# Hybrid decoder step on one core: who copies the second own strides, where head 2's rotation and head 3's sums stand, and the order of the first softmax work

## The chip, the cores and the metric

The kernel runs on one core of a Trainium2 chip. The metric is the device time of one execution in microseconds. Before the change three executions took 855.06, 856.63 and 857.32 us, median 856.63 us.

## What is computed

One layer of a decoder trunk for 512 prompt tokens and 64 sample tokens (8 sequences of 8, each with 1024 cached rows): a root-mean-square norm, one input projection, a convolution branch and a sparse attention branch, their gated sum, then a mixture of 32 experts. What the change touches lies in the attention branch: the rotation of the queries, and the compression of raw keys and values.

```python
def rope(x, pos):
    ...
    return jnp.concatenate([x1 * cos - x2 * sin, x2 * cos + x1 * sin], axis=-1).astype(x.dtype)

def compress(k_raw, w1, b1, w2):
    ...
    pre = jnp.einsum('bnlgd,lde->bnge', s[:, 0:nb], w1r[0]) + b1
    for r in range(1, CMP_RATIO):
        pre = pre + jnp.einsum('bnlgd,lde->bnge', s[:, r:r + nb], w1r[r])
    return jnp.einsum('bnge,ef->bngf', jax.nn.silu(pre), w2)
```

Compression runs twice, first for keys and then for values. Each time 16-row strides are multiplied by two matrices (w1), neighbouring strides are added, a silu follows, and a second small matrix (w2). The attention then takes compressed scores (31 per query in the prompt), selected blocks and a window. Each of the eight query heads is rotated for the last two.

## The kernel before, in words

Every engine has its own program, written by hand. What passes from TensorE through PSUM to VectorE or ScalarE is a job in one list, ORDER (lines 66 to 75). There are four PSUM slots of 1024 columns, and a job's place in the list modulo four is its slot. claim (a wait of TensorE) lets a job start when the job four places earlier has been emptied, take waits for it to be filled, and result_of waits for it to be emptied. So the order of the list, and each engine's own order, set who waits for whom.

The jobs around the change are these:

- raw (n, u), with n = 0 for keys and 1 for values: TensorE turns half a block of 128 cached strides (raw_turned, L1964). Four copies of 64x512 put the result into XT (spread, L819). For n = 1 VectorE copies u = 4 and u = 6, and ScalarE the other six.
- own (n): the prompt's own 32 strides are turned (own_turned, L1973) and copied in four pieces of 64x256 (spread_own, L827). ScalarE copies them for n = 0 and VectorE for n = 1.
- w1 and w1own (n): compress_first multiplies the cached strides (32 matmul instructions at L1983, 512 columns each) and the own ones (32 at L1989, 32 columns each). It waits until raw 4 to 7 and own are copied. ScalarE copies the upper half out (upper_halves, L1069 and L1072), VectorE adds (compress_pre, L1417 and L1424), ScalarE applies silu (compress_silu, L1076). w2 is the second product (L2040 and L2041 for keys, L2058 for values; w2own is at L2063).
- q (c): queries projects a pair of heads, c from 0 to 3 (L1886); ScalarE copies it out (L1081, L1082). "Head c" below is this pair.
- rope (c): TensorE permutes the queries (rotated, L2001). VectorE makes two products (L1431, L1433, the second empties the slot) and two sums: L1435 writes the prompt's rotated queries qrot, L1436 the samples' qs. All rotations share the scratch tile qtmp.

The convolution is VectorE's: conv (L1376) for the prompt, conv_sample (L1402, L1404) in eight steps of one multiplication and one reduction for the samples, and its bias (L1408). SyncE and GpSimd wait for the end of the convolution (conv_done) before they start loads for the stage after the attention (GpSimd's first is L943).

The prompt's attention starts when the last four jobs before it are empty. TensorE computes the compressed scores (cmp_scores, L2128 and L2130) and the scores of units 0 and 1 (L2094, L2097); there are 24 units, six to a head. VectorE takes the compressed maxima (cmp_maxima, L1523, L1524), the units' maxima (maxima, L1498) and the compressed sums and weights (cmp_normalize, L1528 to L1532), and weights the units' probabilities (normalize, L1503 to L1508). ScalarE takes exponentials (L1136 and L1131). cmp_turns (L2136) needs cmp_normalize; behind it TensorE computes unit 2's scores and then turns unit 0's probabilities (L2107). A unit's scores need qrot of its head only, and head 3 comes with unit 18. qs is read by GpSimd after the whole attention.

Of the kernel before, what the change touches and what calls it, by code (L numbers as in the profile page):

```python
# [20 lines left out]
SEQ, DB, DS = 512, 8, 8  # L21
# [41 lines left out]
def mg_jobs(n0, n1):  # L63
# [4 lines left out]
ORDER += [("gs", 0), ("ga", 0), ("raw", 0, 0), ("kt", 0), ("gs", 1), ("raw", 0, 1), ("ga", 1), ("raw", 0, 2), ("kt", 1),  # L68
          ("gs", 2), ("raw", 0, 3), ("ga", 2), ("raw", 0, 4), ("gs", 3), ("raw", 0, 5), ("ga", 3), ("raw", 0, 6), ("raw", 0, 7), "cso"]
ORDER += [("own", 0), ("q", 0), ("w1", 0), ("w1own", 0), ("raw", 1, 0), ("raw", 1, 1), ("q", 1), ("w2", 0), ("rope", 0),  # L70
          ("raw", 1, 2), ("raw", 1, 3), ("q", 2), ("raw", 1, 4), ("raw", 1, 5), ("rope", 1), ("raw", 1, 6), ("raw", 1, 7), ("own", 1), ("rope", 2),
          ("w1", 1), ("w1own", 1), ("q", 3), ("w2", 1), "w2own", ("rope", 3)]
J_ATT = len(ORDER)
ORDER += [("keys", 0, 0), ("keys", 0, 1)] + mg_jobs(0, 4) + ["mean"] + mg_jobs(4, 8) + [("keys", 0, 2)] + mg_jobs(8, 10) + ["var"] + mg_jobs(10, 22)
ORDER += [("small", 0), ("mg", 22), ("mg", 23), ("pcn", 0), ("mg", 24), ("imp", 0), ("mg", 25), ("head", 0), ("mg", 26)]
# [12 lines left out]
JOB = {name: n for n, name in enumerate(ORDER)}  # L88
# [37 lines left out]
def build(nc, a):  # L126
    o = a["outs"]
    with ExitStack() as ctx:
# [36 lines left out]
        def take(eng, *jobs, it=None, per=0):  # L165

            highest(eng, filled, [want(j, it, per, 1) for j in jobs])

        def result_of(eng, *jobs, it=None, per=0):

            highest(eng, emptied, [want(j, it, per, 1) for j in jobs])
# [4 lines left out]
        def give(ins, j):  # L176
            ins.then_inc(emptied[home_of(j)[0]], 1)
# [644 lines left out]
        def spread_own(copy, how, j):  # L822

            for q in range(2):
                for g in range(NKV):
                    v = slot(j)[g * HD:(g + 1) * HD, 0:512].rearrange("p (k q s) -> p k q s", q=2, s=STR_P)[:, :, q, :]
                    last = copy(XT[q * HD:(q + 1) * HD, g, :, STR_S:STR], v, *how)  # L827
            return last
# [199 lines left out]
        def _(act):  # L1028
# [26 lines left out]
            def spread_raw(n, *us):  # L1055
                for u in us:
                    j = JOB["raw", n, u]
                    take(act, j)
                    give(spread(nc.scalar.activation, (ACT.Copy,), j, u), j)
# [6 lines left out]
            def upper_halves(n):  # L1066
                j = JOB["w1", n]
                take(act, j)
                nc.scalar.activation(upper[:, :, 0:STR_S], slot(j)[HD:P, :].rearrange("p (g n) -> p g n", g=NKV), ACT.Copy).then_inc(s_upper, 1)  # L1069
                j = JOB["w1own", n]  # L1070
                take(act, j)
                nc.scalar.activation(upper[:, :, STR_S:STR], slot(j)[HD:P, 0:2 * STR_P].rearrange("p (g n) -> p g n", g=NKV), ACT.Copy).then_inc(s_upper, 1)  # L1072
# [19 lines left out]
            j = JOB["cso"]  # L1092
# [9 lines left out]
            spread_raw(1, 2, 3)  # L1102
            queries(2)
            spread_raw(1, 5, 7)
            upper_halves(1)
            compress_silu(1)
            queries(3)
# [203 lines left out]
        def _(dve):  # L1311
# [75 lines left out]
            def spread_raw(n, u):  # L1387
                j = JOB["raw", n, u]
                take(dve, j)
                give(spread(V.tensor_copy, (), j, u), j)  # L1390

            def conv_sample(t0, t1):

                if t0 == 0:
                    dve.wait_ge(s_anew, CC)
                    result_of(dve, JOB["ga", CC - 2], JOB["ga", CC - 1])
                weights = wdw[:, :, :].unsqueeze(2).to_broadcast([P, CC, DB, TAPS])
                new = cv[:, :, SEQ:T].rearrange("p c (b t) -> p c b t", t=DS)
                for t in range(t0, t1):
                    if t:  # L1400
                        dve.wait_ge(s_prod, 2 * t)
                    V.tensor_tensor(cprod, aS[:, :, :, t:t + TAPS], weights, ALU.mult).then_inc(s_prod, 1)  # L1402
                    dve.wait_ge(s_prod, 2 * t + 1)
                    V.tensor_reduce(new[:, :, :, t], cprod, AX.X, ALU.add).then_inc(s_prod, 1)  # L1404
                if t1 == DS:
                    dve.wait_ge(s_prod, 2 * DS)
                    for c in range(CC):
                        V.tensor_scalar(cv[:, c, SEQ:T], cv[:, c, SEQ:T], bdw[:, c:c + 1], None, ALU.add).then_inc(s_conv, 1)  # L1408

            def compress_pre(n):  # L1410
                j = JOB["w1", n]
                dve.wait_ge(s_pads, 3)
                take(dve, j)
                dve.wait_ge(s_upper, 2 * n + 1)
                for g in range(NKV):
                    lo = slot(j)[0:HD, g * 512:(g + 1) * 512].rearrange("p (b n) -> p b n", b=DB)
                    last = V.scalar_tensor_tensor(pre[:, g, 0:STR_S].rearrange("p (b n) -> p b n", b=DB)[:, :, 0:NCS], lo[:, :, 0:NCS], b1[:, n:n + 1],  # L1417
                                                  upper[:, g, 0:STR_S].rearrange("p (b n) -> p b n", b=DB)[:, :, 1:NCS + 1], ALU.add, ALU.add)
                give(last, j)
                j = JOB["w1own", n]  # L1420
                take(dve, j)
                dve.wait_ge(s_upper, 2 * n + 2)
                for g in range(NKV):
                    last = V.scalar_tensor_tensor(pre[:, g, STR_S:STR_S + NCP], slot(j)[0:HD, g * STR_P:g * STR_P + NCP], b1[:, n:n + 1],  # L1424
                                                  upper[:, g, STR_S + 1:STR_S + 1 + NCP], ALU.add, ALU.add)
                give(last, j)

            def rotated(c):
                j = JOB["rope", c]
                result_of(dve, JOB["q", c])  # L1430
                st.do(V.tensor_tensor(qtmp[:, 1, :], qT[:, c, :], cosT[:, :], ALU.mult))  # L1431
                take(dve, j)
                give(V.tensor_tensor(halves(qtmp[:, 0, :]), tokens(j), halves(sinT[:, :]), ALU.mult), j)  # L1433
                result_of(dve, j)
                V.tensor_tensor(qrot[:, c, :], qtmp[:, 0, 0:SEQ], qtmp[:, 1, 0:SEQ], ALU.add).then_inc(s_qrot, 1)  # L1435
                st.do(V.tensor_tensor(qs[:, 1, c, :], qtmp[:, 0, SEQ:T], qtmp[:, 1, SEQ:T], ALU.add))  # L1436

            j = JOB["cst"]
            take(dve, j)
# [35 lines left out]
            rotated(0)  # L1475
            conv(3, 22, TAPS)
            spread_raw(1, 4)
            rotated(1)
            spread_raw(1, 6)
            j = JOB["own", 1]  # L1480
            take(dve, j)
            give(spread_own(V.tensor_copy, (), j), j)
            rotated(2)
            conv_sample(0, 5)
            compress_pre(1)
            conv_sample(5, DS)
            j = JOB["w2own"]
            take(dve, j)
            for g in range(NKV):
                r = slice(g * STR_P, (g + 1) * STR_P)  # L1490
                last = V.tensor_copy(vcB[r, g * HD:(g + 1) * HD], slot(j)[r, g * HD:(g + 1) * HD])
            give(last, j)
            rotated(3)

            def maxima(u):
                x = unit[u]
                dve.wait_ge(s_score, u + 1)
                V.tensor_reduce(x.stat(0), x.by_branch(x.scores), AX.X, ALU.max, negate=True).then_inc(s_max, 1)  # L1498
# [27 lines left out]
            def cmp_normalize(c):  # L1526
                dve.wait_ge(s_cexp, c + 1)
                st.do(V.tensor_reduce(cstat[c][:, 1, :], Pc[c % 2], AX.X, ALU.add))  # L1528
                st.do(V.reciprocal(cstat[c][:, 1, :], cstat[c][:, 1, :]))
                g = gates[:, 0:QT, :].rearrange("p q (g c r) -> p q g c r", g=NKV, c=HPG)[:, :, :, c, 0]  # L1530
                st.do(V.tensor_tensor(cstat[c][:, 2, :].rearrange("p (q g) -> p q g", g=NKV), cstat[c][:, 1, :].rearrange("p (q g) -> p q g", g=NKV), g, ALU.mult))
                V.tensor_tensor(Pc[c % 2], Pc[c % 2], wide_c(cstat[c][:, 2, :]), ALU.mult).then_inc(s_cnorm, 1)  # L1532

            cmp_maxima(0)
            maxima(0)
            maxima(1)
            cmp_normalize(0)
            normalize(0)
            for u in range(NU):
                if u + 2 < NU:  # L1540
                    maxima(u + 2)
                if u + 1 < NU:
                    normalize(u + 1)
                if u % PER_C == 2 and u // PER_C + 1 < HPG:
                    cmp_maxima(u // PER_C + 1)
                probs_turned(u)
                if u % PER_C == 4 and u // PER_C + 1 < HPG:
                    cmp_normalize(u // PER_C + 1)
# [328 lines left out]
        def _(pe):  # L1877
# [89 lines left out]
            def own_turned(n):  # L1967
                j = JOB["own", n]
                src = (raw[0], raw_own)[n]
                pe.wait_ge(*((s_raw[0], 48) if n == 0 else (s_own, 16)))  # L1970
                claim(pe, j)
                for k in range(16):
                    last = tr(slot(j)[:, k * STR_P:(k + 1) * STR_P], src[0:STR_P, k, :], ident[0:STR_P, 0:STR_P])  # L1973
                fill(last, j)
# [72 lines left out]
            rotated(1)  # L2047
            raw_turned(1, 6, 7)
            own_turned(1)
            rotated(2)  # L2050
            compress_first(1)
            queries(3)
            j = JOB["w2", 1]
            pe.wait_ge(s_silu, 2)
# [457 lines left out]
```

## Time and profile before

| | before |
|---|---|
| median of 3 executions | 856.63 us |
| the profiled execution | 858.87 us |
| its span, first to last instruction | 857.0 us |
| mean granted TensorE clock | 0.951 |
| TensorE busy | 754.0 us (88%) |
| VectorE busy | 380.0 us (44%) |
| ScalarE busy | 220.8 us (26%) |
| GpSimd busy | 167.0 us (19%) |

Times in the trace are microseconds from the first instruction. In the rows PE is TensorE's matrix products, PEld its weight loads, DVE VectorE, ACT ScalarE, POOL GpSimd and SP SyncE. "x16" is a count of instructions merged into a row, and a bracket at its end tells how long the engine was idle before it and what ended that. The granted clock is a share of full speed, so 0.50 is the lower of TensorE's two levels. The stage that the change touches lies between 185 and 250 us.

### The profile page before, as it was taken

How to read it: one execution, taken by the hardware profiler on the slowest of the kernel's cores; microseconds unless marked ns; L12 is line 12 of the kernel's file. 1: busy time of each engine (PE TensorE's matmuls, PEld its weight loads, DVE VectorE, ACT ScalarE, POOL GpSimd, SP SyncE). 2: the span in 40 equal slices, each digit the busy share in tenths (PEclk: the TensorE clock that was granted, in tenths of full speed). 3: DMA queues.
4: the chain of work that ended last, by engine and by line, in shares of the span. 5: the costliest groups of instructions: out<-in, count | busy, mean ns of one | idle time of the engine just before them, and what ended most of it. 6: DMA issues, size and time to landing. Idle time of an engine off the chain costs nothing.

```text
span 857.0 us, 11122 instructions
## 1 busy us (share of the span) xinstructions
PE 754.0 (88%) x4270; PEld 518.1 (60%) x4270; DVE 380.0 (44%) x799; ACT 220.8 (26%) x480; POOL 167.0 (19%) x270
## 2 busy tenths in 40 slices
PE   5999999998899989999999979999996499987730
PEld 3557787774666667777777657774454365554410
DVE  2213999898778861030045532222137432221118
ACT  3001233350356651251244420000010122212113
POOL 2449265000200014000024210001000223221100
PEclk9999999999999999999999999999997699999975
DMA  9766354220540005432234279104007699999836
GB/s 315 152 32 198 101 122 146 63 73 1 168 166 2 1 26 174 132 102 61 74 98 150 79 208 396 43 0 136 24 26 306 239 370 412 406 400 395 313 127 250
DMA packets 87567, 138.95 MB, mean 162 GB/s; under 512 B 25493, under 2 KB 60465, under 8 KB 86351
## 3 DMA queue, kind: packets, MB, share of 16 engines
q1 hardware_dynamic: 71503, 101.41, 34.5%
q0 software_dynamic: 11392, 32.71, 12.9%
q10 hardware_dynamic: 4616, 4.08, 1.5%
q8 instruction: 36, 0.59, 0.3%
q14 instruction: 20, 0.16, 0.1%
HBM read 132.00 MB, written 21.14 MB: 179 GB/s over the span
## 4 chain that ended last, share of the span: by engine, by line
PE 76%; DMA 10%; DVE 7%; issue 4%; SPq 2%; ACT 2%; another core or an unknown queue 0%; POOL 0%; DVEq 0%; POOLq 0%; ACTq 0%
PE ps L1886 18%; PE ps L2076 14%; PE ps L2322 6%; PE ps L2393 5%; PE ps L1910 5%; DMA keep<-w_up 4%; PE ps L1983 3%; PE ps L2409 2%; DMA arena<-w_up 2%; PE ps L2119 2%; PE ps L2107 2%; PE ps L2094 2%; PE ps L1964 2%; PE ps L2383 1%; PE ps L2174 1%
## 5 line engine op out<-in xcount | busy, mean ns | idle before, releaser
L2076 PE MATMUL ps<-xT,keep 128*128 128x288 f32 x512 | 126.9, 407 | 0.9 <-ACT h L1190 0.5
L2076 PEld LDWEIGHTS ps<-xT,keep 128*128 128x128 f32 x512 | 96.5, 190 | 27.6 <-ACT h L1190 0.9
L1886 PE MATMUL ps<-xT,arena 128*128 128x288 f32 x384 | 95.4, 407 | 0.0
L1376 DVE SCALAR_TENSOR_TENSOR cv<-keep,cv 128x512 f32<-128x512 f32 x120 | 83.6, 747 | 1.4
L1886 PEld LDWEIGHTS ps<-xT,arena 128*128 128x128 f32 x384 | 72.1, 190 | 19.2
L2322 PE MATMUL ps<-arena,xT 128*128 128x512 f32 x128 | 55.5, 593 | 1.8 <-issue 1.8
L2393 PE MATMUL ps<-keep,mgT 128*64 128x256 f32 x288 | 44.1, 406 | 9.2 <-DMA keep<-w_up 6.3
L2393 PE MATMUL ps<-arena,mgT 128*64 128x256 f32 x256 | 39.9, 397 | 4.4 <-DMA xT<-w_up 3.0
L1910 PE MATMUL ps<-mgT,xT 128*128 128x512 f32 (+1 forms) x128 | 43.2, 497 | 0.0
L2322 PEld LDWEIGHTS ps<-arena,xT 128*128 128x128 f32 x128 | 24.1, 190 | 31.4 <-issue 31.4
L1260 ACT ACTIVATE keep<-h 128x1024 f32<-128x1024 f32 (+1 forms) x5 | 5.3, 1058 | 140.3 <-DVE h L1687 131.7
L819 ACT ACTIVATE mgT<-ps 64x512 f32<-64x512 f32 x56 | 33.1, 591 | 32.0 <-PE ps L1964 31.4
L1007 POOL DMA_INDIRECT yscratch<-cv,slots_of x19 | 19.0, 999 | 109.2 <-PE ps L2383 76.7
L2393 PEld LDWEIGHTS ps<-keep,mgT 128*64 128x64 f32 x288 | 27.5, 146 | 19.7 <-issue 11.7
L1886 PE MATMUL ps<-cv,keep 128*128 128x288 f32 x128 | 34.6, 426 | 5.3 <-DMA arena<-w_nsa_out 5.3
L1837 DVE TENSOR_TENSOR arena<-ps,cv 128x128 f32<-128x128 f32 x19 | 5.5, 292 | 73.1 <-ACT cv L1275 73.1
L962 POOL TENSOR_SCALAR keep<-keep,pmod 128x64 f32<-128x64 f32 x16 | 6.8, 443 | 157.0 <-PE ps L2119 85.2
L1910 PEld LDWEIGHTS ps<-mgT,xT 128*128 128x128 f32 x128 | 24.1, 190 | 18.1 <-issue 14.8
L1114 ACT ACTIVATE mgT<-ps 128x288 f32<-128x288 f32 x32 | 13.1, 410 | 79.6 <-PE ps L2076 76.1
L1886 PEld LDWEIGHTS ps<-cv,keep 128*128 128x128 f32 x128 | 25.6, 201 | 12.9 <-issue 5.4
L1131 ACT ACTIVATE arena<-ps,arena 128x128 f32<-128x128 f32 (+3 forms) x64 | 32.9, 528 | 1.7 <-DVE arena L1498 0.9
L1275 ACT ACTIVATE cv<-ps 128x128 f32<-128x128 f32 x19 | 5.3, 277 | 108.1 <-PE ps L2393 108.1
(387 smaller groups left out, 1275.0 us busy)
## 6 DMA issues: line engine op xcount, KB each, us to landing
arena<-w_down SPq DMA_DIRECT2D x21, 512.0 KB
keep<-w_gate SPq DMA_DIRECT2D x18, 512.0 KB
keep<-w_up SPq DMA_DIRECT2D x18, 512.0 KB
keep<-w_in SPq DMA_DIRECT2D x16, 512.0 KB, 3.9
arena<-w_gate SPq DMA_DIRECT2D x14, 512.0 KB
arena<-w_up SPq DMA_DIRECT2D x14, 512.0 KB
h<-x_prompt SPq DMA_DIRECT2D x8, 512.0 KB, 7.6
arena<-w_in SPq DMA_DIRECT2D x8, 512.0 KB, 8.0
```

Source lines behind the costliest of these rows:

```text
L819: last = copy(XT[q * HD:(q + 1) * HD, g, k0:k0 + KD // 2, (u // 2) * P:(u // 2 + 1) * P], v, *how)
L1007: pool.indirect_dma_start(a["yscratch"][0:2 * T, :], bass.IndirectOffsetOnAxis(ap=slots_of[:, 1, blocks_of(p):blocks_of(p) + 1], axis=0), ...
L1131: nc.scalar.activation(x.prob[:, g, k], x.scores[:, g, k], ACT.Exp, bias=x.stat(0)[:, g, b:b + 1], accum_out=x.stat(1)[:, g, b:b + 1]).the ...
L1376: V.scalar_tensor_tensor(cv[:, c, 0:SEQ], aP[:, c, k:k + SEQ], wdw[:, c, k:k + 1], cv[:, c, 0:SEQ], ALU.mult, ALU.add).then_inc(s_tap[c], 1)
L1886: last = mm(tokens(j)[:, b, :], weights(k), halves(x[:, k, :])[:, b, :], start=k == 0, stop=k == n_k - 1)
L1910: last = mm(slot(j)[:, lo:hi], xT[:, k, i * P:(i + 1) * P], wkv[:, k, lo:hi], start=k == 0, stop=k == KD - 1)
L1964: last = tr(slot(j)[:, k * P:(k + 1) * P], raw[r % 2][:, (u % 2) * KD + k, :], ident[:, :])
L1983: last = mm(slot(j)[:, g * 512:(g + 1) * 512], w1[:, k, :], XT[:, g, k, 0:STR_S], start=k == 0, stop=k == KD - 1)
L2076: last = mm(out[:, 0:half], wmg[n // 2 % 3][:, k, :], xT[:, k, (n % 2) * half:(n % 2 + 1) * half], start=k == 0, stop=k == KD - 1, skip_gr ...
L2094: mm(x.scores[:, g, b * x.nk:(b + 1) * x.nk], qrot[hd, x.c, qc], kT[hd, br, 0:x.nk], start=b == 0, stop=False, skip_group_check=True)
L2322: last = mm(slot(j)[:, lo:lo + 512], xT[:, k, i * P:(i + 1) * P], wo[:, k, lo:lo + 512], start=k == 0, stop=k == KD - 1)
L2393: last = mm(slot(j + 1)[u * BR:(u + 1) * BR, 0:2 * F], xeT[p % 2][:, k, u * BR:(u + 1) * BR], wgu[(2 * p + u) % HOMES_W][:, :, k, :], star ...
```

## The change

- The own value strides (own 1) are copied by ScalarE, behind its raw (1, 7); VectorE's copies go.
- VectorE copies raw (1, 6) before head 1's rotation, not behind it. It runs six steps of the sample convolution, not five, before compress_pre(1), and only then head 2's rotation.
- TensorE permutes head 2 behind compress_first(1), in the job list too.
- Head 3's rotation is split: its two products stay, its two sums move to the attention, behind normalize(0).
- At the entry of the attention cmp_normalize(0) stands before maxima(1), not behind it.

```diff
--- before.py
+++ after.py
@@ -68,8 +68,8 @@
 ORDER += [("gs", 0), ("ga", 0), ("raw", 0, 0), ("kt", 0), ("gs", 1), ("raw", 0, 1), ("ga", 1), ("raw", 0, 2), ("kt", 1),
           ("gs", 2), ("raw", 0, 3), ("ga", 2), ("raw", 0, 4), ("gs", 3), ("raw", 0, 5), ("ga", 3), ("raw", 0, 6), ("raw", 0, 7), "cso"]
 ORDER += [("own", 0), ("q", 0), ("w1", 0), ("w1own", 0), ("raw", 1, 0), ("raw", 1, 1), ("q", 1), ("w2", 0), ("rope", 0),
-          ("raw", 1, 2), ("raw", 1, 3), ("q", 2), ("raw", 1, 4), ("raw", 1, 5), ("rope", 1), ("raw", 1, 6), ("raw", 1, 7), ("own", 1), ("rope", 2),
-          ("w1", 1), ("w1own", 1), ("q", 3), ("w2", 1), "w2own", ("rope", 3)]
+          ("raw", 1, 2), ("raw", 1, 3), ("q", 2), ("raw", 1, 4), ("raw", 1, 5), ("rope", 1), ("raw", 1, 6), ("raw", 1, 7), ("own", 1),
+          ("w1", 1), ("w1own", 1), ("rope", 2), ("q", 3), ("w2", 1), "w2own", ("rope", 3)]
 J_ATT = len(ORDER)
 ORDER += [("keys", 0, 0), ("keys", 0, 1)] + mg_jobs(0, 4) + ["mean"] + mg_jobs(4, 8) + [("keys", 0, 2)] + mg_jobs(8, 10) + ["var"] + mg_jobs(10, 22)
 ORDER += [("small", 0), ("mg", 22), ("mg", 23), ("pcn", 0), ("mg", 24), ("imp", 0), ("mg", 25), ("head", 0), ("mg", 26)]
@@ -1102,6 +1102,7 @@
             spread_raw(1, 2, 3)
             queries(2)
             spread_raw(1, 5, 7)
+            spread_raw_own(1)
             upper_halves(1)
             compress_silu(1)
             queries(3)
@@ -1425,15 +1426,21 @@
                                                   upper[:, g, STR_S + 1:STR_S + 1 + NCP], ALU.add, ALU.add)
                 give(last, j)
 
-            def rotated(c):
+            def rotated_parts(c):
                 j = JOB["rope", c]
                 result_of(dve, JOB["q", c])
                 st.do(V.tensor_tensor(qtmp[:, 1, :], qT[:, c, :], cosT[:, :], ALU.mult))
                 take(dve, j)
                 give(V.tensor_tensor(halves(qtmp[:, 0, :]), tokens(j), halves(sinT[:, :]), ALU.mult), j)
-                result_of(dve, j)
+
+            def rotated_sum(c):
+                result_of(dve, JOB["rope", c])
                 V.tensor_tensor(qrot[:, c, :], qtmp[:, 0, 0:SEQ], qtmp[:, 1, 0:SEQ], ALU.add).then_inc(s_qrot, 1)
                 st.do(V.tensor_tensor(qs[:, 1, c, :], qtmp[:, 0, SEQ:T], qtmp[:, 1, SEQ:T], ALU.add))
+
+            def rotated(c):
+                rotated_parts(c)
+                rotated_sum(c)
 
             j = JOB["cst"]
             take(dve, j)
@@ -1475,22 +1482,19 @@
             rotated(0)
             conv(3, 22, TAPS)
             spread_raw(1, 4)
+            spread_raw(1, 6)
             rotated(1)
-            spread_raw(1, 6)
-            j = JOB["own", 1]
-            take(dve, j)
-            give(spread_own(V.tensor_copy, (), j), j)
+            conv_sample(0, 6)
+            compress_pre(1)
             rotated(2)
-            conv_sample(0, 5)
-            compress_pre(1)
-            conv_sample(5, DS)
+            conv_sample(6, DS)
             j = JOB["w2own"]
             take(dve, j)
             for g in range(NKV):
                 r = slice(g * STR_P, (g + 1) * STR_P)
                 last = V.tensor_copy(vcB[r, g * HD:(g + 1) * HD], slot(j)[r, g * HD:(g + 1) * HD])
             give(last, j)
-            rotated(3)
+            rotated_parts(3)
 
             def maxima(u):
                 x = unit[u]
@@ -1533,9 +1537,10 @@
 
             cmp_maxima(0)
             maxima(0)
+            cmp_normalize(0)
             maxima(1)
-            cmp_normalize(0)
             normalize(0)
+            rotated_sum(3)
             for u in range(NU):
                 if u + 2 < NU:
                     maxima(u + 2)
@@ -2047,8 +2052,8 @@
             rotated(1)
             raw_turned(1, 6, 7)
             own_turned(1)
+            compress_first(1)
             rotated(2)
-            compress_first(1)
             queries(3)
             j = JOB["w2", 1]
             pe.wait_ge(s_silu, 2)
```

## Rows read from the trace of the kernel before

**Rows 1.** The page, part 4: shares of the chain that ended last.

```profile
PE 76%; DMA 10%; DVE 7%; issue 4%; SPq 2%; ACT 2%; another core or an unknown queue 0%; POOL 0%; DVEq 0%; POOLq 0%; ACTq 0%
```

**Rows 2.** The same chain in order of time, 140 to 260 us: start, duration, what.

```profile
145.57 13.73 PE ps L1983 x32
...
162.96 3.27 PE ps L1964 x16
...
176.26 1.75 PE ps L1964 x16
...
196.72 15.61 PE ps L1983 x32
212.33 3.49 PE ps L1989 x32
...
234.46 1.06 PE ps L2136 x4
235.52 1.58 PE ps L2094 x4
...
255.72 0.44 PE ps L2136 x4
...
257.18 0.84 PE ps L2094 x4
```

**Rows 3.** Waits, 140 to 260 us: waiting instruction, releaser, total, times, longest.

```profile
POOL arena L943 <- DVE cv L1408: 46.1, 1, 46.1
...
PE ps L1983 <- DVE mgT L827: 3.8, 1, 3.8
...
PE ps L2136 <- DVE arena L1532: 2.6, 1, 2.6
```

**Rows 4.** Timeline of VectorE, 190 to 248 us.

```profile
189.51 0.76 DVE L1431 TENSOR_TENSOR arena<-h,keep 128x576 f32<-128x576 f32 x1
...
191.95 2.79 DVE L819 COPY mgT<-ps 64x512 f32<-64x512 f32 x4
194.78 1.73 DVE L827 COPY mgT<-ps 64x256 f32<-64x256 f32 x4
...
198.99 1.19 DVE L1402 TENSOR_TENSOR arena<-keep 128x992 f32<-128x992 f32 x1
...
225.95 0.44 DVE L1491 COPY keep<-ps 32x64 f32<-32x64 f32 x2 [1.38 <-PE ps L2063]
```

**Rows 5.** Timeline of ScalarE, 140 to 245 us.

```profile
190.66 2.40 ACT L819 ACTIVATE mgT<-ps 64x512 f32<-64x512 f32 x4 [0.71 <-PE ps L1964]
```

**Rows 6.** The copies at L827 over the whole run: duration min/median/max.

```profile
L827 ACT ACTIVATE mgT<-ps x4: 361/376/380, 140.6 to 141.8; 64x256 f32<-64x256 f32 x4
```

**Rows 7.** Timeline of TensorE's products, 140 to 250 us.

```profile
190.56 1.18 PE L1973 MATMUL ps<-ident,arena 32*128 32x32 f32 x16
191.66 1.24 PE L2001 MATMUL ps<-h,keep 128*128 128x288 f32 x4
```

**Rows 8.** Stretches: length, busy PE, PEld, DVE, ACT, POOL, granted clock, DMA share, GB/s.

```profile
196.72:200.10 3.38, 3.38 (x4) 1.48 (x5) 3.28 (x5) 0.00 (x0) 0.00 (x0) 0.51 0.02 5
...
234.20:237.60 3.40, 3.14 (x12) 1.61 (x13) 1.46 (x8) 1.79 (x7) 0.00 (x0) 0.50 1.13 430
```

**Rows 9.** Timeline of all engines, 227.5 to 238 us.

```profile
228.00 0.69 DVE L1435 TENSOR_TENSOR h<-arena 128x512 f32<-128x512 f32 x1
...
231.35 1.82 DVE L1498 TENSOR_REDUCE arena<-ps 128x4 f32<-128x512 f32 x2 [0.59 <-PE ps L2097]
...
233.97 0.43 DVE L1532 TENSOR_TENSOR arena<-arena 128x256 f32<-128x256 f32 x1
...
234.72 0.87 DVE L1508 TENSOR_SCALAR arena<-arena 128x128 f32<-128x128 f32 x4
234.80 0.51 ACT L1131 ACTIVATE arena<-ps,arena 128x256 f32<-128x256 f32 x1
...
237.46 0.96 DVE L1498 TENSOR_REDUCE arena<-ps 128x2 f32<-128x768 f32 x1 [1.87 <-PE ps L2097]
```

## The prediction

> **What bounds the kernel now.** I read the chain that ended last first, for the engine that must get faster: TensorE holds 76% of it, VectorE 7% [rows 1]. Then the chain in order of time, to see where it leaves TensorE near the change. In the stage from 185 to 250 us the second compress product starts at 196.72 and takes 15.61 us, the own strides' part 3.49 [rows 2]. The waits say why it did not start sooner: 3.8 us on VectorE's last copy of own strides, the longest wait of TensorE here [rows 3]. The second place is the attention's entry: cmp_turns waits 2.6 us on cmp_normalize [rows 3], and later VectorE waits 1.87 us for unit 2's scores [rows 9]. The granted clock comes last, because it changes what an idle gap costs. It was 0.51 in the first 3.38 us of the product and 0.50 from 234.2 to 237.6, both times behind a stretch with no matrix product [rows 8]. The same 32 instructions took 13.73 us for keys [rows 2], so that fall cost 15.61 - 13.73 = 1.88 us. The one at the entry slowed the compressed turns and unit 2's scores to 1.06 + 1.58 = 2.64 us, where the same four turns and four 384-column score products took 0.44 + 0.84 = 1.28 for later units at full clock [rows 2]. That fall cost about 1.36.
>
> **The own copies and the product's start.** VectorE now does head 1's rotation (189.51 to 191.95, 2.44 us), raw (1, 6) (2.79) and the own copies (1.73), and is done at 196.5 [rows 4]. After the change it does raw (1, 6) from 189.51, which TensorE has turned by then (its next job on the same engine, own, starts at 190.56 [rows 7]), to 192.34, and the rotation to 192.34 + 2.44 = 194.78. ScalarE finishes raw (1, 7) at 190.66 + 2.40 = 193.06 [rows 5]. The own strides are turned at 190.56 + 1.18 = 191.74 [rows 7], so its four copies follow at once, and take 4 x 0.376 = 1.5 us, the time of the key strides' copies on ScalarE [rows 6], where VectorE's took 1.73 [rows 4]: done by 194.6. ScalarE has nothing queued behind them before the upper half of this same product, so nobody pays for its 1.5 us. The list moves too: w1 (1) now takes the slot of rope (1), which head 1's rotation empties with its second instruction, before 194.78. The product can start at about 194.85. **Term one: 194.85 - 196.72 = -1.9 us.**
>
> **Head 2's permutation.** It lies in the idle gap today, 191.66 to 192.9 [rows 7], and costs nothing. Behind the product TensorE is never idle, so its four matrix instructions come onto the path. **Term two: +1.2 us** (1.24 by its row). VectorE's side stays covered. Six sample steps are twelve instructions of 1.2 us [rows 4], so they are done near 194.8 + 14.6 = 209.4. The product ends at 194.85 + 15.6 = 210.5 or, at full clock, 194.85 + 13.7 = 208.6, and ScalarE's copy of its upper half comes between it and compress_pre. VectorE is thus late by under 0.8 us at worst, and it waits 1.38 us before w2own's copy today [rows 4]. That slack also hides head 2's rotation behind the product, which takes 2.44 us while one sample step (2.4 us) has moved ahead. If the cover went, w2own's copy, head 3's two products and the attention's start would be late one for one. In the list rope (2) takes raw (1, 7)'s slot, long empty, and q (3) keeps own's; no new slot wait falls on TensorE.
>
> **Queues.** No DMA moves in program order. GpSimd's gathers and SyncE's loads wait for the end of the convolution (GpSimd 46.1 us [rows 3]), which comes some 1 to 2 us earlier, and are used only after the attention. Price zero. Their traffic then lies against the attention's entry a little differently; TensorE reads nothing of it there.
>
> **The attention's entry.** maxima(0) and (1) fill 231.35 to 233.17, cmp_normalize ends at 234.40, normalize(0) at 235.59 [rows 9]. Unit 1's maximum reads twice the columns of unit 0's, some 1.1 of the 1.82 us. With cmp_normalize ahead of it, cmp_turns starts at about 233.35 rather than 234.46: -1.1 us for TensorE. VectorE's sum of work to the end of normalize(0) is the same, 235.59. Now the two sums of head 3 come, about 0.85 us from start to start (L1435 begins at 228.00 and took 0.69 [rows 9]; L1436 is the 64-column one, which I put at 0.2). So maxima(2) can start at 236.45. At the low clock it started at 237.46, held by TensorE [rows 9]; TensorE now has the scores at about 236.4, so both are ready together. The gain here is 237.46 - 236.45 = 1.0 us. Where the sums stood before, VectorE had to wait for TensorE anyway, so taking them away there gives nothing, and ScalarE's exponentials of unit 1, which ended at 234.80 + 0.51 = 235.3 [rows 9], end about 1 us later, still before maxima(2) is through and unit 1 is normalized. At the full clock the old order would have started maxima(2) at 237.46 - 1.36 = 236.1, and the new one still at 236.45, because VectorE now sets it: +0.35. **Term three: between -1.0 (low clock, as profiled) and +0.35 (full clock).** Which holds in a typical execution the trace cannot say; I take -0.3, half way.
>
> **The sum.** Against the profiled execution: -1.9 + 1.2 - 1.0 = -1.7, so 858.87 - 1.7 = 857.2 us with the clock's falls kept, and 855.3 if the product no longer starts slow. That execution stands 2.24 us above the median of 856.63, about what one or two such falls cost, so the typical execution probably has fewer. Against the median: -1.9 + 1.2 - 0.3 = -1.0, and the idle gap before the product shrinks from 3.8 us to 194.85 - 191.74 = 3.1. A gap of 2.6 us was enough for a fall at the entry [rows 3, 8], so 3.1 is not safe. I give the shorter gap a quarter of 1.88, some -0.4. That makes 856.63 - 1.4 = **855.2 us**. What follows the attention is tied to TensorE's progress (weights are requested when it frees their place), so the shift should arrive at the end.
>
> **A rule of the skill.** The low clock stands behind gaps of 3.8 and 2.6 us [rows 3, 8]. The Trainium skill (TensorE: Matmul & The Clock Gate, The HAM clock gate) says that "the default state is throttled, and activity releases the throttle". By that rule alone a change which shortens both gaps should keep the clock up more often; the trace agrees that falls follow gaps, and has no gap of the new lengths.
>
> **Rivals.**
>
> *Both falls vanish.* The typical execution had the fall before the product and the new one has not: -1.9 + 1.2 - 1.88, and the entry anywhere in its term, gives -2.6 - 0.3 = -2.9, so 853.7. For it: the gap shrinks by a fifth, the entry's by 1.1 of 2.6. Against it: 855.06 was the fastest of three executions, and if falls were absent there, there is nothing to gain. Chance 0.20.
>
> *The copies were not the last wait.* Something else holds the product, such as the slot that rope (1) has to leave, or ScalarE behind raw (1, 7). If VectorE's rotation starts late by 1 us, the start is 195.8, and terms one and two cancel. With the entry at +0.35 it comes out at 856.6 to 857. For it: three events (194.6, the slot, the turned strides) now meet within 1 us. Against it: each is shorter than 1.9 us late. Chance 0.15.
>
> *Slower: the clock falls in another place.* The clock fell once behind the narrow 32-column products of the keys: the next turns took 3.27 us, against 1.75 for the same 16 later, 1.5 us lost [rows 2]. In the values' run the same kind of products (3.49 us [rows 2]) were followed by full speed. Started 2 us earlier they may be the place of a fall, with head 2's permutation and head 3's query product behind them at the low level: half of a stretch like the 3.4 us of [rows 8], +1.7. With the entry at full clock that is -0.7 + 1.7 + 0.35 = +1.35 us, 858.0. It makes the change a loss as soon as more than 0.7 us is lost there, and a measurable one only where the low level lasts two such stretches: -0.7 + 3.4 + 0.35 = +3.05, 859.7. Chance 0.08, and 0.04 for the second form.
>
> **How the numbers follow.** The forecast has 0.57, the rivals 0.20, 0.15 and 0.08. A measurement of this kernel can tell about 0.3%, or 2.6 us, from no change. The forecast's bounds are -0.7 - 1.0 - 0.9 = -2.6 and -0.7 + 0.35 = -0.35, that is 854.0 to 856.3; the three executions before differ by 2.3 us among themselves. To hold 8 in 10 the range takes in most of the first two rivals: 853.3 to 857.1, with the last of its width for the scatter of a median. Faster by over 0.3% is the first rival, 0.20. Slower by over 0.3% is the third in its second form, 0.04. Within 0.3% is the rest, 0.76.
>
> **What would show it.** Right: L827 runs on ScalarE at about 193.1 to 194.6; L1983 waits about 3.0 us, on ScalarE, and starts near 194.9; L2001 stands behind L1989 and takes 1.2 us; w2own's copy starts 0.7 us earlier or, with the product at full clock, 2.6; the gap before L2136 is near 1.6 us; L1435 of head 3 stands behind the first L1508 and directly before the third L1498, with little wait between. Wrong: the product's wait ends on VectorE, at L1433; L1402 reaches past the product's end; VectorE is late at w2own; or the granted clock is down in a stretch where it was up.

## The result, and the profile after

The changed kernel takes 861.26 us, the median of 20 executions; the kernel before takes 858.23 us, also over 20. The ratio is 1.0031, with a 95% interval of 1.0018 to 1.0045: slower by about 0.3%, 2.6 us. The forecast was 855.2 us, its range 853.3 to 857.1. The value lies above the range, and the direction is wrong. (The 856.63 us that the forecast started from was the median of three executions, 1.6 us below that of 20.)

First, the changed kernel's page: the span, busy time, and the granted clock in 40 slices. TensorE's busy time grew from 754.0 to 758.5 us for the same 4270 products, and slices 10, 12 and 24 (193 to 214, 236 to 257 and 493 to 514 us) are no longer at 9, as all of the first 30 were before. The first two lie in the stage of the change.

```profile
span 857.5 us, 11122 instructions
...
PE 758.5 (88%) x4270; PEld 519.9 (61%) x4270; DVE 378.2 (44%) x795; ACT 222.2 (26%) x484; POOL 167.9 (20%) x270
...
PEclk9999999998979999999999989999997599999875
```

**What came as forecast.** Two waits of the changed kernel (columns as in [rows 3]; the first is forecast, the second, before unit 1's turns, is not and comes up below), and the timelines of ScalarE and VectorE ahead of the product. They answer to [rows 3], [rows 4] and [rows 5].

```profile
PE ps L1988 <- ACT mgT L827: 3.1, 1, 3.1
...
PE ps L2112 <- DVE arena L1519: 2.2, 2, 1.6
```

```profile
190.20 2.40 ACT L819 ACTIVATE mgT<-ps 64x512 f32<-64x512 f32 x4 [0.90 <-PE ps L1969]
192.62 1.54 ACT L827 ACTIVATE mgT<-ps 64x256 f32<-64x256 f32 x4
```

```profile
186.23 5.61 DVE L819 COPY mgT<-ps 64x512 f32<-64x512 f32 x8
191.87 0.76 DVE L1432 TENSOR_TENSOR arena<-h,keep 128x576 f32<-128x576 f32 x1
```

ScalarE copies the own strides in 1.54 us, right behind raw (1, 7), and they end TensorE's wait, which is 3.1 us now. Now the chain in order of time, which answers to [rows 2]:

```profile
194.38 16.22 PE ps L1988 x32
210.60 3.49 PE ps L1994 x32
214.09 1.05 PE ps L2006 x4
215.14 7.76 PE ps L1891 x32
```

The product starts 2.3 us earlier, but takes 16.22 us rather than 15.61, and head 2's permutation stands in the chain behind it. At 215.14 head 3's query product starts, 0.7 us earlier than the 215.82 of before. This profiled execution was 0.45 us ahead already where VectorE began raw (1, 4) (186.23 here, 186.68 before), so little of the first two terms is left.

**Where the time went.** VectorE at the attention's entry, which answers to [rows 9]:

```profile
229.74 0.69 DVE L1502 TENSOR_REDUCE arena<-ps 128x4 f32<-128x512 f32 x1
230.34 0.41 DVE L1532 TENSOR_REDUCE arena<-arena 128x8 f32<-128x256 f32 x1
...
234.61 0.69 DVE L1438 TENSOR_TENSOR h<-arena 128x512 f32<-128x512 f32 x1
235.22 0.22 DVE L1439 TENSOR_TENSOR keep<-arena 128x64 f32<-128x64 f32 x1
235.47 0.96 DVE L1502 TENSOR_REDUCE arena<-ps 128x2 f32<-128x768 f32 x1
```

cmp_normalize (L1532) follows unit 0's maximum, and the two sums (L1438, L1439) stand right in front of unit 2's maximum, with no wait between. That is the forecast's order. TensorE in the same stretch, after and then before (the bracket is the idle time ahead of a group):

```profile
227.36 0.41 PE L2133 MATMUL ps<-keep,h 128*128 128x64 f32 x2 [1.05 <-DVE arena L1434]
...
229.63 2.08 PE L2099 MATMUL ps<-keep,h 64*128 64x256 f32 x8
...
235.62 0.92 PE L2099 MATMUL ps<-keep,h 64*128 64x384 f32 x4 [0.42 <-ACT arena L1132]
...
238.36 1.06 PE L2112 MATMUL ps<-ident,arena 128*128 128x128 f32 x8 [1.61 <-DVE arena L1519]
...
241.93 2.08 PE L2099 MATMUL ps<-keep,h 64*128 64x512 f32 x4
```

```profile
228.12 0.41 PE L2128 MATMUL ps<-keep,h 128*128 128x64 f32 x2 [1.05 <-DVE arena L1433]
...
230.38 1.14 PE L2094 MATMUL ps<-keep,h 64*128 64x256 f32 x8
...
237.93 0.92 PE L2094 MATMUL ps<-keep,h 64*128 64x384 f32 x4
...
240.35 1.07 PE L2107 MATMUL ps<-ident,arena 128*128 128x128 f32 x8 [1.30 <-DVE arena L1515]
...
242.99 1.13 PE L2094 MATMUL ps<-keep,h 64*128 64x512 f32 x4
```

The wait that matters is the one before unit 1's turns (L2112 after, L2107 before): 1.61 us for 1.30. It ends on L1519, VectorE's copy of unit 0's turned probabilities, which in VectorE's order stands behind the two sums, unit 2's maximum and the weighting of unit 1. The turns still start 2.0 us earlier than before. But unit 4's scores, four matrix instructions of 512 columns, then take 2.08 us where they took 1.13. The stretches by the clock, before and after (columns as in [rows 8]):

```profile
180.00:200.00 20.00, 16.01 (x84) 11.69 (x83) 18.34 (x29) 7.45 (x14) 0.00 (x0) 0.92 0.17 53
...
240.00:250.00 10.00, 9.65 (x88) 6.39 (x88) 7.50 (x18) 4.53 (x13) 0.00 (x0) 1.00 0.40 147
```

```profile
180.00:200.00 20.00, 16.53 (x82) 11.48 (x81) 19.33 (x26) 8.33 (x17) 0.00 (x0) 0.83 0.11 46
...
240.00:250.00 10.00, 10.00 (x56) 6.63 (x56) 4.16 (x10) 3.29 (x11) 0.00 (x0) 0.50 0.37 141
```

From 240 to 250 us the clock is at its lower level throughout, where the kernel before had full speed, and in ten microseconds TensorE gets through 56 instructions rather than 88. This profile also has an earlier fall, from about 229.8 to 233.2 us, ahead of the waits discussed here: unit 1's scores (the eight instructions of 256 columns above) took 2.08 us for 1.14. The end of the attention, as the start of the merge gates in the chain (before, then after):

```profile
320.30 15.52 PE ps L2076 x64
```

```profile
323.01 15.52 PE ps L2081 x64
```

From the first compressed scores to this point: 320.30 - 228.12 = 92.18 us before, 323.01 - 227.36 = 95.65 after. The changed kernel entered the attention 0.8 us earlier and left it 2.7 us later. Its span ends only 0.5 us behind, because the profiled execution of before lost 2.9 us in the sample pairs (445 to 494 us), partly to a wait on a queue that the trace does not name; the profiles of the changed kernel and of every experiment take 46.7 us for the same stretch, that one 49.6. Why is open. One pair of profiles is therefore not enough, and the experiments go by 12 executions each and by the mean granted clock that every execution reports.

### The profile page after: what moved, and what is told of

It is laid out like the page before. It is cut to its first block, busy times and chain, and to the rows that moved or that the text cites. A ratio compares the mean times of both kernels' runs of the same rounds, so it can differ in the third digit from the quotient of the medians.

```text
span 857.5 us, 11122 instructions
## 1 busy us (share of the span) xinstructions
PE 758.5 (88%) x4270; PEld 519.9 (61%) x4270; DVE 378.2 (44%) x795; ACT 222.2 (26%) x484; POOL 167.9 (20%) x270
## 4 chain that ended last, share of the span: by engine, by line
PE 79%; DMA 8%; DVE 6%; issue 3%; SPq 2%; ACT 1%; ACTq 0%; DVEq 0%; POOLq 0%
PE ps L1891 18%; PE ps L2081 15%; PE ps L2398 6%; PE ps L2327 6%; PE ps L1915 5%; PE ps L1988 3%; PE ps L2414 3%; PE ps L2124 2%; DMA arena<-w_up 2%; PE ps L2099 2%; PE ps L2112 2%; DMA keep<-w_up 2%; PE ps L2388 2%; PE ps L2179 1%; PE ps L1969 1%
## 6 DMA issues: line engine op xcount, KB each, us to landing
arena<-w_down SPq DMA_DIRECT2D x21, 512.0 KB, 16.8
```

## The experiments

Each kernel ran 12 times, in three sets on three chips, with 35 executions of the kernel before in each set (medians 859.64, 858.60 and 858.34 us). "Mean" and "clock" are averages over a kernel's executions of the time and of the granted clock. The kernel before has a clock of 0.9462, 0.9465 and 0.9466 in the three sets and means of 859.45, 858.78 and 858.75 us. The standard error of a mean is 0.4 to 0.8 us.

| kernel | median us | ratio to before (95%) | mean minus before's | clock |
|---|---|---|---|---|
| changed, first measurement | 861.26 | 1.0031 (1.0018 to 1.0045) | +2.6 | 0.9427 |
| e1: entry order alone | 856.55 | 0.9969 (0.9951 to 0.9988) | -3.2 | 0.9492 |
| e2: deferred sums alone | 858.95 | 1.0006 (0.9983 to 1.0029) | +0.3 | 0.9453 |
| e3: the product's part alone | 858.78 | 0.9993 (0.9971 to 1.0015) | -0.3 | 0.9444 |
| e4: both entry edits | 861.21 | 1.0030 (1.0007 to 1.0052) | +1.9 | 0.9437 |
| e5: changed, sums put back | 857.24 | 0.9980 (0.9960 to 1.0001) | -1.6 | 0.9461 |
| e6: changed, sums later | 856.13 | 0.9972 (0.9954 to 0.9991) | -2.6 | 0.9477 |
| e7: changed, gap filled | 856.37 | 0.9974 (0.9954 to 0.9995) | -2.3 | 0.9492 |
| e8: e5, product's gap filled | 855.99 | 0.9963 (0.9942 to 0.9983) | -3.0 | 0.9497 |
| e9: own copies and entry order | 855.65 | 0.9961 (0.9943 to 0.9978) | -3.0 | 0.9479 |
| e10: e9, product's gap filled | 855.42 | 0.9965 (0.9949 to 0.9980) | -3.5 | 0.9487 |
| e11: e10, entry gap filled too | 855.14 | 0.9958 (0.9940 to 0.9977) | -4.0 | 0.9497 |
| e12: changed, again | 861.30 | 1.0036 (1.0015 to 1.0056) | +2.8 | 0.9417 |

(One execution of e6, at 1344.45 us, is left out of its mean and its clock. Its median has it.)

**First set: the parts alone.** Theory A was that the new order of the entry lets the clock fall, B that the sums do, C that the product's part does.

e1, only the order of the entry:

```diff
             maxima(0)
+            cmp_normalize(0)
             maxima(1)
-            cmp_normalize(0)
             normalize(0)
```

> Alone: cmp_normalize(0) ahead of maxima(1). Theory A (the new order of the entry leaves TensorE idle before unit 1's turns, and the granted clock falls there and stays down for some 10 us): slower than before by 2 to 5 us, mean granted clock over the runs lower by about 0.006, and the profile shows a low stretch between 235 and 260 us. Theory B (the head 3 sums on VectorE do it): within 1 us of before. Theory C (the product's part does it): within 1 us of before.

Theory A as stated is refuted: this edit alone makes the kernel faster by 3.2 us, and the mean clock is higher, 0.9492 for 0.9462. TensorE's timeline:

```profile
228.44 0.41 PE L2128 MATMUL ps<-keep,h 128*128 128x64 f32 x2 [1.05 <-DVE arena L1433]
...
237.89 1.06 PE L2107 MATMUL ps<-ident,arena 128*128 128x128 f32 x8 [0.78 <-DVE arena L1515]
```

Unit 1's turns start 9.45 us behind the first compressed scores, for 12.23 before, and the wait ahead of them is 0.78 us. cmp_turns starts 4.34 us behind them (232.78), for 6.34 before: 2.0 us earlier, where the forecast had 1.1. Part of that is a wait which [rows 9] does not show, because both maxima are merged in one row. In e3, which keeps the old order, VectorE waits 0.70 us between unit 0's maximum and unit 1's, for unit 1's scores:

```profile
232.39 1.23 DVE L1496 TENSOR_REDUCE arena<-ps 128x4 f32<-128x1024 f32 x1 [0.70 <-PE ps L2095]
```

The new order puts cmp_normalize(0) into that wait.

e2, only the deferral (rotated(3) split, and the sums behind normalize(0)):

```diff
-            rotated(3)
+            rotated_parts(3)
...
             normalize(0)
+            rotated_sum(3)
```

> Alone: head 3's two sums behind normalize(0). Theory A: within 1 us of before. Theory B: slower than before by 2 to 5 us with a lower mean clock, because maxima(2) and all of unit 1 come 0.3 to 0.9 us later and TensorE idles meanwhile. Theory C: within 1 us.

Level with before (+0.3 us). In the old order VectorE waited there for TensorE (1.87 us before unit 2's maximum, [rows 9]), and the sums fit into that wait. Theory B, the sums by themselves, falls too. The profile of e2 is one of its slowest executions (861.34 us): it has a long fall of the clock, 0.50 from 230.3 to 240.6 us, so such a fall can come without both edits. In the mean it did not show: the clock is 0.9453 for 0.9462.

e3, everything but the two entry edits (the job list, own copies on ScalarE, raw (1, 6) first, head 2 behind the product, six sample steps):

```diff
+            spread_raw_own(1)
...
-            rotated(2)
             compress_first(1)
+            rotated(2)
```

> Everything of the change but the two edits at the attention's entry: own copies on ScalarE, raw (1, 6) first, head 2's permutation behind the product, six sample steps. Theories A and B: faster than before by 0.7 to 2 us, mean clock equal to before's. Theory C (the narrow products or head 2's place bring the clock down): slower by 2 us or more with a lower mean clock.

Level with before (-0.3 us), so theory C falls. The forecast of -0.7 for this part is within its error (0.6). Its mean clock is the lower one, 0.9444 for 0.9462.

e4, both entry edits and nothing else:

> Only the two edits of the attention's entry. Theories A and B: slower than before by 3 to 5 us, mean clock 0.942 to 0.946 as in the changed kernel (0.943). Theory C: within 1 us of before.

Slower, with a mean clock near the changed kernel's. So the loss is neither edit's alone. Their effects alone add up to -2.9 us; together they give +1.9. The difference of 4.8 us (standard error about 1.1) is their interaction.

```profile
228.94 0.41 PE L2135 MATMUL ps<-keep,h 128*128 128x64 f32 x2 [1.05 <-DVE arena L1433]
...
239.22 1.49 PE L2114 MATMUL ps<-ident,arena 128*128 128x128 f32 x8 [1.61 <-DVE arena L1521]
```

```profile
240.00:250.00 10.00, 10.00 (x62) 5.47 (x60) 4.94 (x13) 3.46 (x11) 0.00 (x0) 0.67 0.62 223
```

Against e1 the turns come 10.28 - 9.45 = 0.83 us later, about what the two sums take (0.85 us from start to start), and the wait ahead of them is 1.61 instead of 0.78. The delay explains 0.83 of the 4.8 us. For the rest the clock was the suspect: 0.9437 against 0.9492. As an estimate, that difference of 0.0055 over a span of 857 us is 4.7 us of full clock.

**Second set: delay or clock.** The same edit undone or moved, and then the delay kept and the idle time filled.

e5, the changed kernel with `rotated(3)` whole again, ahead of the attention:

> The changed kernel with head 3's sums back where they were (all other edits kept). Theory A (the sums in front of maxima(2) leave TensorE idle 1.6 us before unit 1's turns, and the granted clock then falls and stays low for 7 to 10 us in most executions): faster than before by 3 to 4 us, mean clock 0.948 or more, idle before unit 1's turns about 0.8 us. Theory B (the sums only add their own 0.85 us, the rest is the product's part): within 1.5 us of before, mean clock near 0.944.

e6, the changed kernel with the sums where VectorE waited for unit 4's scores:

```diff
-            rotated_sum(3)
             for u in range(NU):
+                if u == 2:
+                    rotated_sum(3)
```

> The changed kernel with head 3's sums right before maxima(4), where VectorE waited 1.65 us for TensorE in the kernel before. Theory A: like the kernel with the sums back, 2 to 4 us faster than before, because the place and not the deferral is what costs. Theory A2 (any deferred sum in the attention costs): within 1 us of before or slower.

Both recover the loss and stand below before (-1.6 and -2.6 us). So deferring costs nothing; the place does. e5 gained less than the 3 to 4 us expected. Its clock is 0.9461, and in its profile the clock fell at 237.5 us behind a wait of only 0.78: without the sums the fall is rarer, not gone.

e7 is the test of the clock. It keeps every edit of the change, and adds work, six transposes whose result nobody uses:

```diff
+                if u == 1:
+                    for n in range(6):
+                        tr(obank[:, n % 4 * P:(n % 4 + 1) * P], ident[:, :], ident[:, :])
                 turns(u)
```

> The changed kernel with twelve idle transposes (six pairs, about 1.3 us at full clock, into a PSUM bank not in use) between the scores of unit 3 and the turns of unit 1, where TensorE idles 1.6 us. They compute nothing that is used. Theory A, clock: mean clock up by 0.004 or more against the changed kernel's 0.943, and the time 2 to 3 us lower, that is level with before or below, though work was added. Theory B: no faster than the changed kernel, which was 2.6 to 3 us slower than before.

The expectation counts two transposes to each turn of the loop. The trace has one: six instructions, 0.82 us together, not twelve and 1.3.

```profile
228.45 0.41 PE L2133 MATMUL ps<-keep,h 128*128 128x64 f32 x2 [1.05 <-DVE arena L1434]
...
236.97 0.82 PE L2163 MATMUL ps<-ident 128*128 128x128 f32 x6
...
238.73 1.06 PE L2112 MATMUL ps<-ident,arena 128*128 128x128 f32 x8 [0.94 <-DVE arena L1519]
```

```profile
240.00:250.00 10.00, 9.38 (x91) 5.99 (x91) 7.53 (x18) 5.63 (x16) 0.00 (x0) 1.00 0.39 147
```

Unit 1's turns start 10.28 us behind the first compressed scores, to the hundredth as late as in e4. The delay is untouched. Yet the stage from 240 to 250 runs at full clock, the mean clock is 0.9492, and the kernel is 2.3 us faster than before, some 5 us faster than the changed kernel. The attention's end in the chain, e1 and then e7:

```profile
317.81 15.52 PE ps L2076 x64
```

```profile
318.65 15.52 PE ps L2081 x64
```

From the first compressed scores that is 89.37 us in e1, 90.20 in e7 (0.83 more, the sums), and 95.65 in the changed kernel. So of the changed kernel's surplus over e1, 0.83 us is delay and 5.4 is the clock in that execution. Of these 5.4 us, 0.7 belong to the earlier fall at 229.8: the turns of unit 1 start 11.00 us behind the first compressed scores there, for 10.28 in e4 and e7. From these turns on, the attention takes 79.92 us in e1 and in e7, 83.06 in e4, 84.65 in the changed kernel and 85.94 in its second profile (e12).

This shows the cause: with the same delay and more work, the time and the clock both come back. It does not show how long a wait is harmless (e5's clock fell behind 0.78 us, e1's and e6's did not), nor how often a fall comes, since there is one profile of each kernel.

e8 puts ten idle transposes (again not pairs) into the gap ahead of the product of e5:

```diff
             own_turned(1)
+            claim(pe, JOB["w1own", 1])
+            for n in range(10):
+                tr(slot(JOB["w1own", 1])[:, n % 8 * P:(n % 8 + 1) * P], ident[:, :], ident[:, :])
             compress_first(1)
```

> The kernel with the sums back, plus twenty idle transposes (ten pairs, about 2.1 us at full clock) in the 3 us gap before the second compress product. They compute nothing that is used. Clock theory: the product starts at full clock in nearly all executions (13.7 us rather than 15.6 to 16.2), so 1 to 2 us faster than the kernel with the sums back, 4 to 6 us faster than before. If the product's low stretches were only chance: no difference to the kernel with the sums back.

The product, in e5 and then in e8 with the transposes (L2056) ahead of it:

```profile
194.81 16.64 PE L1987 MATMUL ps<-mgT,arena 128*128 128x512 f32 x32 [3.11 <-ACT mgT L827]
```

```profile
192.98 1.31 PE L2056 MATMUL ps<-ident 128*128 128x128 f32 x10 [0.63 <-DVE mgT L819]
195.46 13.97 PE L1987 MATMUL ps<-mgT,arena 128*128 128x512 f32 x32 [1.17 <-DVE arena L1434]
```

It takes 13.97 us instead of 16.64, and the kernel is another 1.4 us faster than e5 (standard error 0.6), within the 1 to 2 us expected of the filling. Against before it is 3.0 us, not the expected 4 to 6.

**Third set: a version that beats both.** e9 takes only the own copies on ScalarE with raw (1, 6) first, and the entry's order. Head 2's permutation stays ahead of the product.

> Two parts of the change only: own copies on ScalarE with raw (1, 6) first, and cmp_normalize ahead of maxima(1). Head 2's permutation stays ahead of the product, head 3's sums stay put. If head 2's permutation behind the product costs its 1.2 us: about 1 us faster than the kernel with the sums back, 2.5 to 4.5 us faster than before, TensorE's permutation at about 194 in the former gap and the product at about 195.2. If its place is worth nothing: level with the kernel with the sums back (1.4 us faster than before).

-3.0 us; against e5, from which it differs in head 2's place (and in one sample step of VectorE), -1.4 (standard error 0.8). Permuting head 2 in the gap is at least not worse, and the figure is near the 1.2 us of term two. e10 adds seven idle transposes (0.99 us) ahead of the permutation, e11 three more ahead of unit 1's turns:

> The kernel of the run before, plus fourteen idle transposes (seven pairs, 1.5 us at full clock) in the gap before head 2's permutation. They compute nothing that is used. Clock theory: product at full clock, 13.7 to 14 us, 1 to 2.5 us faster than without them, mean clock 0.949 or more, and 5 us or more faster than the changed kernel. Otherwise no difference.

> The same, plus six idle transposes (three pairs, 0.65 us) in the 0.8 us gap before unit 1's turns. Clock theory: as fast or up to 1 us faster, mean clock a little higher, scatter smaller. Otherwise no difference.

They come out at -3.5 and -4.0 us, each 0.5 from the one before and inside the error. In e10's profile the clock fell ahead of the product all the same, so that filling did not do what was expected of it. All three profiles (e9, e10, e11) have a second fall, right behind the 32-column products of the own strides, where head 3's query product runs. In e10 (columns as in [rows 8]):

```profile
214.40:217.80 3.40, 3.40 (x9) 2.40 (x8) 3.16 (x5) 1.18 (x2) 0.00 (x0) 0.51 0.00 0
```

This is the place that the prediction's third rival named. None of the other eleven profiles has a fall there. Why it moved there was not tried. e11 is the fastest kernel measured here, but its lead over e9 and e1 is not shown.

e12 repeats the changed kernel in the third set:

> The changed kernel as it is, on the same chip as the three others: 0.2 to 0.4% slower than before, mean clock 0.941 to 0.944, and 3 to 5 us slower than the kernels above. If it comes out level with before, the slowdown first measured was chance.

The slowdown repeats: +2.8 us, 1.0036 (1.0015 to 1.0056). Its profile has the low stretch again:

```profile
240.00:250.00 10.00, 10.00 (x45) 6.01 (x45) 4.77 (x11) 1.83 (x6) 0.00 (x0) 0.50 0.40 146
```

## Why the prediction was wrong

- **The own copies and the product's start** (-1.9): right in mechanism. ScalarE copies in 1.54 us and is the last releaser, the wait is 3.1 us as worked out. The start came near 194.8 to 195.2 in most profiles.
- **Head 2's permutation** (+1.2): stands in the chain behind the product, as worked out, with 1.05 us in the chain.
- **The quarter of 1.88 us for the shorter gap**: wrong in sign. The clock still fell in the 3.1 us gap. In half-microsecond stretches it was low for 6.8 us around the product's start in all six profiles with the new product part and no filling (the changed kernel twice, e3, e5, e6, e7), and the product took 16.2 to 16.8 us. Of the four with the old part, three had 3.4 us (15.4 to 15.7 us for the product) and e4 6.8 (16.9). That takes back about 1 us, and what the two terms left could not be measured (e3).
- **The attention's entry** (term three, between -1.0 and +0.35): this is the step that failed. The order of VectorE was right (the sums directly ahead of maxima(2), without a wait). But the term followed only maxima(2) and the wait before cmp_turns. That wait did shrink, to 0.62 us in e4 and e12, below the 1.6 that was worked out (and to nothing in the first profile of the changed kernel, where unit 1's scores ran at the low clock and filled it). The premise that VectorE comes to the end of normalize(0) no earlier was wrong too: in e1 the weighting of unit 0 starts 5.74 us behind the first compressed scores, for 6.60 before, mostly because cmp_normalize fills the wait between the two maxima. Above all, the term did not follow the next wait of TensorE, before unit 1's turns. With TensorE earlier by the new order and VectorE later by the sums, that wait became the longest there, 1.61 us. It had no row in the prediction and no bound. What it cost was not its own length but a fall of the clock for 7 to 14 us (e4, the changed kernel, e12) in an attention that is TensorE's path: from the turns on, 3.1, 4.7 and 6.0 us in these three profiles against e7. The two edits were priced as one sum; their interaction of 4.8 us was the result. The prediction's own last sign of being wrong, a granted clock that is down in a stretch where it was up, is what the profile shows from 240 to 250 us.
- **The rival "slower: the clock falls in another place"** had the right kind of mechanism and the wrong place for this kernel: behind the own strides' narrow products its two profiles show no fall, though those of e9 to e11 do. Its chance of 0.08 covered one place and not the others.
- **The rule on the clock.** The prediction concluded that a change which shortens both gaps should keep the clock up more often. The rule behind it, that activity releases the throttle, is that of the Trainium skill (TensorE: Matmul & The Clock Gate, The HAM clock gate), and e7 agrees with it: six idle transposes alone took the mean clock from 0.9427 to 0.9492. The conclusion failed because it looked at the two gaps that shrank and not at the one that grew.
- **The base.** The profiled execution was taken for one with more falls than usual, 2.24 us above the median of three. Over 20 executions the median is 858.23, so 858.87 was an ordinary one. That alone moved the forecast by 1.6 us. It is not what made it wrong: from 858.23 the forecast would have been 856.8, still 4.4 below the measured time.

## What to carry to other kernels

When an edit makes the engine on the path ready earlier, follow all of its waits up to the next long job, not only the one that the edit aims at: work deferred "into a wait" is free only as long as that wait is still there. Two edits that touch the same few microseconds are to be measured alone and together. And where a stage alternates between TensorE and a second engine, compare the mean granted clock over many executions: here a wait that grew by 0.8 us went with a loss of 4.8.

## What was not expected of the hardware

Six idle transposes made a kernel some 5 us faster (e7). They took 0.82 us and left 0.94 us of a 1.6 us wait idle, and that was enough. And a fall of the clock in the attention did not end with the next burst of work: TensorE was busy for the whole of 240 to 250 us in the changed kernel, and was at the low level all the while (0.50). Why it stayed there so long was not tried.
